# A two-block transformer kernel: half of the MLP's second product by Strassen's seven products, and the head norm's sums taken between pieces of a product

## The reference, cut to what matters

```python
# first block, after its two attentions
m = rms_norm(h, mlp_norm[i])
h = h + jnp.square(jax.nn.relu(m @ w_mlp_up[i])) @ w_mlp_down[i]     # 1024 -> 4096 -> 1024
gate = jax.nn.sigmoid(rms_norm(h, ple_norm[i]) @ w_ple_gate[i] + b_ple_gate[i])

# second block, differential attention, finish(o, z): of is o by head (8 heads of 128)
of = of * lax.rsqrt(jnp.mean(of * of, axis=-1, keepdims=True) + SUBLN_EPS)
of = of * subln_gain.astype(jnp.float32) * (1.0 - lambda_init)
return (of.reshape(B, L, D).astype(z.dtype) * jax.nn.silu(z)) @ w_out
```

## Time and profile before

| | before |
|---|---|
| median of three runs | 2317.79 us |
| profiled execution, its own time | 2316.58 us |
| its span in the trace | 2314.4 us |
| PE busy | 2206.9 us, 95% |
| DVE / ACT / POOL busy | 54% / 43% / 44% |
| TensorE clock granted, mean | 0.976 |
| first product of the MLP | about 596 to 913 us of the span |
| second product of the MLP | 913 to about 1270 us |
| head norm and projection | about 2150 us to the end |

### The profile page before, as it was taken

The page is one execution under the profiler, slowest core; times in us unless marked ns, Lnnn a source line. Parts: engine busy times, 40 slices in busy tenths (PEclk is TensorE's granted clock), DMA queues, the critical chain, the costliest instruction groups (busy, mean ns, idle before and its releaser), DMA issues. The chain is left out here.

```text
span 2314.4 us, 32355 instructions
## 1 busy us (share of the span) xinstructions
PE 2206.9 (95%) x12108; PEld 1852.5 (80%) x12108; DVE 1258.8 (54%) x2118; ACT 995.3 (43%) x2035; POOL 1018.0 (44%) x863
## 2 busy tenths in 40 slices
PE   6899887999999999999999999999999899999798
PEld 5799746988888888888888878888887788888566
DVE  5555675862776665222225352245411888888645
ACT  6444445872432223312114244333211677777532
POOL 5433342552165555735532244322110677777341
PEclk9999788999999999999999999999999999999899
DMA  5365756631043334523311113367546554451232
GB/s 156 95 168 137 225 199 173 146 99 57 33 132 110 110 110 140 170 73 101 118 55 46 64 37 102 107 208 207 178 137 184 137 136 123 118 143 49 86 121 82
DMA packets 226284, 281.93 MB, mean 122 GB/s; under 512 B 63016, under 2 KB 139192, under 8 KB 226128
## 3 DMA queue, kind: packets, MB, share of 16 engines
q1 hardware_dynamic: 220368, 273.57, 40.5%
q10 hardware_dynamic: 5760, 6.29, 0.8%
HBM read 189.60 MB, written 81.81 MB: 117 GB/s over the span
## 5 line engine op out<-in xcount | busy, mean ns | idle before, releaser
L2975 DVE TENSOR_TENSOR residual<-residual,rm_down 128x512 f32<-128x512 f32 x128 | 87.5, 686 | 231.8 <-PE rm_down L244 231.8
L3684 DVE TENSOR_REDUCE da_low_score<-da_scores 128x1 f32<-128x1280 f32 x128 | 190.0, 1485 | 21.9 <-PE da_scores L3546 21.8
L3665 POOL TENSOR_TENSOR da_prob<-da_prob 128x1280 f32<-128x1280 f32 x64 | 188.8, 2950 | 5.3
L3614 ACT ACTIVATE da_prob<-da_scores,da_low_score 128x1280 f32<-128x1280 f32 x128 | 170.6, 1333 | 13.9 <-DVE da_low_score L3684 13.8
L3663 POOL TENSOR_SCALAR da_prob<-da_prob,da_ratio 128x1280 f32<-128x1280 f32 x64 | 86.0, 1344 | 162.2 <-DVE da_ratio L3692 162.2
L3546 PE MATMUL da_scores<-da_k_hi,da_q 128*128 128x512 f32 (+1 forms) x384 | 149.8, 390 | 5.0 <-ACT da_prob L3614 2.7
L2537 POOL TENSOR_TENSOR rm_w_lo<-rm_stage,rm_w_hi 128x512 fp32r<-128x512 f32 x56 | 73.0, 1314 | 159.8 <-ACT rm_w_hi L2622 159.5
L2557 POOL TENSOR_TENSOR rm_w_lo<-rm_stage,rm_w_hi 128x512 fp32r<-128x512 f32 x64 | 80.8, 1295 | 138.5 <-ACT rm_w_hi L2691 138.5
L3546 PE MATMUL da_scores<-da_k_lo,da_q 128*128 128x512 f32 (+1 forms) x384 | 132.0, 360 | 0.0
L2691 ACT ACTIVATE rm_w_hi<-rm_stage 128x512 fp32r<-128x512 f32 x64 | 38.5, 628 | 194.5 <-PE rm_down L244 159.3
L3699 DVE TENSOR_TENSOR da_aT_lo<-da_turn,da_aT_hi 128x512 fp32r<-128x512 f32 (+1 forms) x192 | 108.9, 595 | 21.1 <-ACT da_aT_hi L3623 18.9
(11 more groups left out here) (571 smaller groups left out, 6918.4 us busy)
## 6 DMA issues: line engine op xcount, KB each, us to landing
rm_stage<-in_w_mlp_up SPq DMA_DIRECT2D x32, 512.0 KB, 4.8
rm_stage<-in_w_mlp_down SPq DMA_DIRECT2D x64, 256.0 KB, 3.1
rm_stage<-inner SPq DMA_DIRECT2D x64, 256.0 KB, 3.0
rm_stage<-in_da_w_in SPq DMA_DIRECT2D x64, 256.0 KB, 3.3
gla_ada_w<-in_ada_w SPq DMA_DIRECT2D x12, 1024.0 KB, 8.2
da_k_hi<-dk_hi SPq DMA_DIRECT2D x32, 320.0 KB, 8.0
da_k_lo<-dk_lo SPq DMA_DIRECT2D x32, 320.0 KB, 9.2
inner<-rm_act_r SPq DMA_DIRECT2D x36, 256.0 KB, 2.0
```

What stands on the lines that cost most here:

```text
L2975: nc.vector.tensor_tensor(c.H[:, t, cols_of(half)], c.H[:, t, cols_of(half)], down_bank[n % 5][:], ALU.add).then_inc(down_added, 1)
L3614: nc.scalar.activation(prob[:, n % BUF, z], scores[z][:, 0:K], ACT.Exp, scale=-1.0, bias=low_score[:, n, z:z + 1], accum_out=sums[:, n, z: ...
L3665: nc.gpsimd.tensor_tensor(p0, p0, p1, ALU.add).then_inc(prob_ready, 1)
L3684: nc.vector.tensor_reduce(out=low_score[:, n, z:z + 1], in_=scores[z][:, 0:K], op=ALU.min, axis=AX.X).then_inc(low_score_ready, 1)
```

## The change

**First product.** For blocks 2 to 13 (`PAIRS`) DVE makes four more tiles from the four results A11, A12, A21, A22 (`inner_sums`): S1 = A21 + A22, S2 = S1 − A11, S3 = A11 − A21, S4 = A12 − S2. Seven tiles of 256 KB are stored instead of four (A21 is not). PE's part is the same.

**Second product** (`DownPlan`). The first four and the last four feature tiles keep the plain scheme, 16 units each. The 24 between are three groups of eight, and each takes seven steps of four units of 12 matmuls, 21 steps in all. A step multiplies a left tile set (A11, S1, A12, S4, S3, S2, A22, four raw tiles from scratch) by a right one (B11, T1, B21, B22, T3, T2, T4, four tiles of `w_mlp_down` or of their differences). The right tiles of a group lie raw in `c.spare` (four loads of 1 MB, `load_right`). ACT makes the high parts of both sides, POOL the low part of the left (`raw_low`), DVE the low part of the right (`right_low`, for the step after next) and the differences T (`right_sum`, three steps ahead, in four of seven steps). A ring of four places holds the parts; all eight banks are used. B21, B22 and T4 go on in the bank of an earlier step. What four quadrants share is kept in four tiles `term` and added at the end (`correct`, 12 additions, which DVE makes after the additions of the 20th step and before those of the 21st and last).

**Head norm.** The eight `add_square` of the second half stand between quarters of `result(0, 1)` and `result(0, 2)`, the roots are covered by five eighths of `result(0, 3)`, and DVE's `roots_low` stands behind the third addition.

```diff
+    PAIRS = range(2, 14)
+    SUMMED = (("A22", 3, 0), ("A11", 4, 1), ("A12", 8, 3), ("S1", 9, 0), ("S2", 10, 1), ("S3", 11, 2), ("S4", 12, 3))
...
+    ORDER = (("A11", "B11"), ("S1", "T1"), ("A12", "B21"), ("S4", "B22"), ("S3", "T3"), ("S2", "T2"), ("A22", "T4"))
+    TERMS = {"T1": ("B12", "T1"), "T3": ("B22", "T3"), "T2": ("B22", "T1"), "T4": ("B21", "T2")}
+    GROUPS, PAIRS, PRODUCTS = 3, 4, 7
...
+        step_bank = up_bank + down_bank
+        last_bank = down_bank[1:5] + down_bank[0:1]
...
+            for q in range(8, RAW):
+                load_raw(q)
+            for what in ("B11", "B12", "B21", "B22"):
+                load_right(0, what)
+            for step in range(STEPS):
+                for j in range(PAIRS):
+                    load_raw(RAW + PAIRS * step + j)
+                g, i = divmod(step, down.PRODUCTS)
+                if i == 6 and g + 1 < down.GROUPS:
+                    load_right(g + 1, "B11")
+                    load_right(g + 1, "B12")
...
+                        if step < 2:
+                            act.wait_ge(unit_done, UNITS)
+                        else:
+                            act.wait_ge(down_ready, down.free(step))
...
+            for step in range(STEPS):
+                for j in range(PAIRS):
+                    raw_high(RAW + PAIRS * step + j)
+                for j in range(PAIRS):
+                    right_high(step, j)
...
+                if b - 1 in up.PAIRS:
+                    dve.wait_ge(inner_stored[1], 16 * up.stored_upto(b - 1, 1))
                 nc.vector.tensor_tensor(second_sum, bank[2], u2, ALU.add).then_inc(post_done, 1)
...
+            def inner_sums(b):
+
+                a22, a11, a21, a12 = squares
+                s1, s2, s4 = first_sum[b % 2], second_sum, unsquared[1]
+                for step, out, x, y, op in ((9, s1, a21, a22, ALU.add), (10, s2, s1, a11, ALU.subtract),
+                                            (11, a21, a11, a21, ALU.subtract), (12, s4, a12, s2, ALU.subtract)):
+                    dve.wait_ge(post_done, up.post(b, 10 if step == 11 else step))
+                    nc.vector.tensor_tensor(out, x, y, op).then_inc(post_done, 1)
...
+            def right_low(step, j):
+
+                dve.wait_ge(right_hi_ready, RIGHT_AT + PAIRS * step + j + 1)
+                nc.vector.tensor_tensor(right_part(step, 1, j), right_raw(step, j), right_part(step, 0, j).bitcast(F32),
+                                        ALU.subtract).then_inc(right_lo_ready, 1)
...
+                    if step + 2 < STEPS:
+                        right_low(step + 2, t)
+                    if step + 3 in down.summed:
+                        right_sum(step + 3, t)
+                if step == STEPS - 2:
+                    correct()
...
+            for step in range(STEPS):
+                what = down.right(step)
+                fresh = what in ("B11", "T1", "T3", "T2")
+                pe.wait_ge(up_lo_ready, OPERANDS + RAW + PAIRS * (step + 1))
+                pe.wait_ge(right_lo_ready, RIGHT_AT + PAIRS * (step + 1))
+                for t in range(PAIRS):
+                    n = down.PLAIN + PAIRS * step + t
+                    pe.wait_ge(down_added, n - 7)
...
+                    chain(step_bank[n % 8][:], terms, fresh, True, down_ready)
...
+                pe.wait_ge(down_added, LAST - 7 + m if m < 4 else LAST if m == 4 else LAST + m - 4)
...
-            result(0, 1)
-            for n in range(DH, N):
-                hn.add_square(pe, n)
+            for h in range(DH):
+                result(0, 1 + h // 4, range(2 * (h % 4), 2 * (h % 4) + 2))
+                hn.add_square(pe, DH + h)
             hn.add_epsilon(pe, 1)
-            result(0, 2)
+            result(0, 3, range(0, 5))
             hn.wide(pe, DH)
             hn.wide(pe, DH + 1)
-            result(0, 3)
+            result(0, 3, range(5, KT))
```

More of the change, by code:

```diff
@@ L2065, in __init__ @@
         self.operands = self.units = len(self.operand)
-        steps = [4 if b < self.WHOLE else 9 for b in range(self.BLOCKS)]
+        steps = [4 if b < self.WHOLE else 13 if b in self.PAIRS else 9 for b in range(self.BLOCKS)]
         self.post_first = [sum(steps[:b]) for b in range(self.BLOCKS + 1)]
@@ L2097, in last_use, with slot_of @@
         return self.unit(self.BLOCKS - 1, [n for n, x in enumerate(self.RIGHT) if x == ("mixed", i)][0]) + 1
+    def slot_of(self, b, i):
+        return i % 2 if b < self.WHOLE else i
     def stores(self, b):
         if b < self.WHOLE:
[L2102 to L2107, removed]
@@ new lines, in first_work, with correct @@
+            def first_work(n):
+                what, j = ("none", "low", "sum", "low")[n // PAIRS], n % PAIRS
+                if what == "low":
+                    right_low(0 if n < 2 * PAIRS else 1, j)
+                elif what == "sum":
+                    right_sum(1, j)
+            def correct():
+                dve.wait_ge(down_added, down.done(STEPS - 2))
+                for t in range(PAIRS):
+                    for row, half in ((t, 1), (t + 4, 0), (t + 4, 1)):
+                        nc.vector.tensor_tensor(c.H[:, row, cols_of(half)], c.H[:, row, cols_of(half)], term[t], ALU.add)\
+                            .then_inc(corrected, 1)
+                dve.wait_ge(corrected, RIGHT_AT + 3 * PAIRS)
@@ L2978, in _ @@
+            for m, (t, half) in enumerate(last_downs):
+                add_to(c.H[:, t, cols_of(half)], LAST + m, last_bank[m % 5])
+                if half:
                     norm_tile(1, t)
@@ new lines, in _ @@
+            for m, (t, half) in enumerate(last_downs):
+                if m == 0:
+                    pe.wait_ge(up_lo_ready, OPERANDS + RAWS)
+                pe.wait_ge(down_added, LAST - 7 + m if m < 4 else LAST if m == 4 else LAST + m - 4)
+                terms = []
+                for j in range(FT):
+                    x, w = ([ring_tile((STEPS + which) % 4, part, HALVES * j + i) for part in range(2)]
+                            for which, i in ((1, t // 4), (0, half)))
+                    terms.append((tuple(y[:, tok_of(t % 4)] for y in x), tuple(w)))
+                product(nc, last_bank[m % 5][:], terms, NCOL, down_ready)
+                if half and t:
```

273 lines of the change are left out of this document (198 added, 75 removed).

## The result

The changed kernel takes **2283.13 us**, the median of four runs (2280.53 to 2284.61), against 2318.18 for the kernel before in the same comparison: a ratio of 0.9846, 95% interval 0.9829 to 0.9863, so 35 us or 1.5% faster. The forecast was 2281, with a range of 2275 to 2296. The profiled execution took 2284.61 us, with a span of 2282.8 and a mean clock of 0.977.

What follows compares the result with a forecast made beforehand. PE, busy 95% of the span, bounds the kernel: matmul count by pace, while other engines keep up. Terms -32.6 + 0 + 0 + 0 + 3 - 7 = -36.6 from 2316.6 give 2280.0, median 2281 us; range 2275 to 2296.

Steps and rivals of the forecast that it cites:

- 1. Matmuls removed: MLP second product: 116 units of 12 matmuls instead of 128, at 2.72 us a unit, take 32.6 us off.
- 2. Inner sums: First product: four more DVE sums in each of 12 blocks, some 3.7 us, fit DVE's idle time; cost 0, bounds 0 to 18.
- the rival of a late S2: First product: S2's store lands late, 1.5 us in each of 12 blocks, giving 2299 us; chance 0.06.
- 5 us of room: First product: slack before PE's sixth unit of a block if the addition waiting for S2's store comes late.
- 3. DVE in the second product: Groups of seven steps: DVE needs about 70 of 76.2 us, so PE is not held; price 0, bounds 0 and 2.4.
- the limit of 1.29: Second product: mean us of DVE's 44 SBUF operations a group past which PE waits for DVE.
- The first rival: Second product: each POOL part holds up a DVE operation for its whole length, 86 us a group, 2310 us; chance 0.13.
- the second: Second product: every DVE SBUF operation takes 1.77 us, 97 us a group of seven steps, 2344 us; chance 0.04.
- 4. Loads: Second product: right and left tiles land before the first step needs them; price 0, bounds 0 and 5 us.
- 5. Corrections: Before the last group's norm: 12 mostly slow additions put scaling 15 us after that group's start (L); PE waits 3 us more.
- My bound of +6: First scaling of the last group: with all 12 corrections slow (21.2 us) it comes at L + 18, costing +6 us.
- 6. Head norm: Head norm sums: squares no longer late and clock kept up, so the first head starts 7 us earlier; bounds 5 and 8.

Runs made afterwards that it cites:

- the five executions with the same wait: Profiled executions with PE waiting 5.7 to 5.8 us: changed kernel twice (2283.13, 2285.80 us), it without new head norm (2289.42), with six (2289.08) or eight (2306.40) inner sums.
- all kernels in the ledger: Profiled executions of old, changed and follow-up kernels, compared between landmarks; from G, first gate and projection product, to the end: mean 1021.6 us with old head norm, 1014.5 with new.

## Why the prediction was right, step by step

**1. Matmuls removed: -32.6.** Right. 12 units went at the old pace; PE stayed full in both products. Of this gain 26.3 us arrive at G: 32.6 and 0.5 of an old wait that is gone, less the 6.7 of step 5, make 26.4.

**2. Inner sums: 0.** Right. They take 3.9 us a block (forecast 3.7), in the DVE timeline of one block:

```profile
765.73 1.77 DVE L3056 SCALAR_TENSOR_TENSOR up_spare<-up_spare 128x512 f32<-128x512 f32 x1
767.53 2.39 DVE L3099 TENSOR_TENSOR up_spare<-up_spare,rm_act_r 128x512 f32<-128x512 f32 x2
769.84 0.68 DVE L3099 TENSOR_TENSOR up_spare<-rm_act_r,up_spare 128x512 f32<-128x512 f32 x1
770.56 0.69 DVE L3099 TENSOR_TENSOR up_spare<-up_spare 128x512 f32<-128x512 f32 x1
...
773.35 0.69 DVE L3070 TENSOR_TENSOR up_spare<-rm_up,up_spare 128x512 f32<-128x512 f32 x1
775.88 0.69 DVE L3087 TENSOR_TENSOR up_spare<-rm_down,up_spare 128x512 f32<-128x512 f32 x1 [1.84 <-PE rm_down L3335]
```

One slow, three fast, as the earlier trace rows let me say, and the square ahead of them starts at 765.73 where it was at 761.93: those 3.8 us are the later start of this whole execution. The addition at 773.35, which waits for the store of S2, has no idle time before it, so the rival of a late S2 did not come; the store lands in 2.1 us. The forecast named "5 us of room" between this addition and PE's sixth unit. That is not what can be filled: by the runs with more sums only 2.0 us a block can, since DVE's own round of a block (busy time and the wait for ACT) fills up first.

**3. DVE in the second product: 0.** Right, with the load overstated: 57 to 60 of 76 us busy, where I had 70. Over the 49.6 us that the forecast gave without POOL, that is 8 to 11 us, 0.3 to 0.4 for each of the 28 low parts of POOL, where I had 20 us, 0.7 each. By group, 965 to 1190 us:

```profile
L3142 DVE TENSOR_TENSOR up_spare<-up_spare 128x512 f32<-128x512 f32 x44 | 46.2, 1050 | 0.3
L3147 DVE TENSOR_TENSOR rm_w_lo<-up_spare,rm_w_hi 128x512 fp32r<-128x512 f32 x36 | 33.8, 938 | 0.0
L3147 DVE TENSOR_TENSOR rm_h_lo<-up_spare,rm_h_hi 128x512 fp32r<-128x512 f32 x20 | 19.7, 986 | 0.0
L3147 DVE TENSOR_TENSOR xb_lo<-up_spare,xb_hi 128x512 fp32r<-128x512 f32 x20 | 19.5, 975 | 0.0
...
L2675 POOL TENSOR_TENSOR rm_w_lo<-rm_stage,rm_w_hi 128x512 fp32r<-128x512 f32 x44 | 65.8, 1526 | 43.0 <-ACT rm_w_hi L2812 43.0
```

The mean of these 120 operations is 119.2 / 120 = 0.99 us, far under the limit of 1.29, and of 1.57 for slower. The first rival, with 86 us of DVE work a group, is refuted, and so is the second. The lock as such is not. The Trainium skill (SBUF — State Buffer, "Who interferes with whom") calls the shared port an exclusive lock. Where both engines had work without a break, the trace fits that: beside POOL's eight parts, which start 1.70 us apart, DVE's corrections start 1.70 us apart too, one for one. Alone they start 0.60 and 1.25 us apart, so a pair takes 0.15 us less than one after the other. Such a meeting costs DVE 1.10 us. In the groups of seven steps it lost only 0.3 to 0.4 us for each part of POOL, where the rival had charged 1.3 for every one.

**4. Loads: 0.** Right. The first low part of a right tile came at 944.41 behind 12.46 us of standing for ACT (forecast: from 927 to 942, and 3.7 us of the difference are the later start), and no PE wait followed.

**5. Corrections: +3. This term was mis-sized; it is 6.7 in this execution.** I took most of the 12 as slow, 18 to 19 us, and scaling at L + 15; they were all slow, 20.1 us, and scaling came at L + 16.0 (L is 1189.5). My bound of +6 for the case of all slow allowed for the wait, which measured 3.9 more than before. What it lacked is that the clock falls behind this wait: 2.8 us more here, 1.9 to 2.8 over the five executions with the same wait. Moving four corrections gave back 6.7 and 6.5 us, as much as the whole term; the old wait of 1.8 went with it, and small later waits came in its place.

**6. Head norm: -7.** Right. The mean over all kernels in the ledger is 7.1. PE's timeline shows no gap among the sums, with a pair of matmuls for a square each 1.84 us (the earlier trace rows has them in one piece, 11.2 us long):

```profile
2204.64 0.39 PE L3633 MATMUL hn_sum<-hn_sq_hi,hn_band 128*8 128x512 f32 x1
2206.49 0.40 PE L3633 MATMUL hn_sum<-hn_sq_hi,hn_band 128*8 128x512 f32 x1
...
2218.11 1.05 PE L3643 MATMUL hn_sum<-ident,da_sums 128*8 128x128 f32 x8
```

The epsilon takes 1.05 us instead of 1.88, since the clock is at 1.00.

**Sum.** Forecast -36.6; the terms measured are -26.3 and -7.1, so -33.4, and the medians say -35 (interval of the ratio: 32 to 40). 2281 missed by 2 us, less than the start of the program wanders, so a part of that closeness is luck: by the ledger the forecast gain is 3.2 us too large, and step 5 alone is 3.7 us short.

## What to carry to other kernels

Before moving work onto a half idle engine, sort its idle time by what ends it: waits for the bottleneck engine are room, waits inside its own chain with a third engine are not (here 2.0 us a block could be filled of the 4 that stood idle). Look for the places where the new work is queued ahead of the one result the bottleneck waits for, and put whatever has a later due time behind it; four additions moved were worth 6.6 us, beside the 35 of the whole scheme. Compare kernels between two landmarks that enclose the change: here that repeats to 0.1 us, while whole runs of one kernel scatter by 4 to 10.

## What the runs showed of the hardware

- A wait of PE can cost more than its length. After 5.7 us the granted clock stood at the 1.2 GHz level (0.50 in a window of 4 us) and 1.9 to 2.8 us more were lost; after 1.8 us (before) and 2.36 us (two corrections moved) it stayed at 1.00. Length alone doesn't decide: of the three waits of 2.63 and 2.64 us with the low parts made twice, the first left the clock at 1.00 (its first matmuls take 0.47 and 0.40 us), while behind the second and the third 7 matmuls each take 0.63 us or more. The window behind the third:

```profile
1192.00:1196.00 4.00, 3.58 (x9) 2.89 (x10) 3.97 (x7) 3.04 (x6) 1.82 (x2) 0.57 0.00 0
```

- The same addition of two SBUF tiles costs DVE 0.64 us with POOL idle (starts 0.60 apart) and 1.70 with POOL making low parts without a break, one operation of each engine every 1.70 us. In a stage where POOL works for 43 of 76 us the mean is 0.99. DVE's additions with one input in PSUM take 0.68 us beside POOL too.
- The unchanged first 520 us of the program differ by up to 5 us from one profiled execution to another. What sets this wasn't examined.
